# Gate and score matmuls of a hybrid decoder layer moved into two 64-row tiles of the array

## What is computed

```python
scores = einsum('bnqhgd,bnkhd->bnhgqk', qb, kc) * 64 ** -0.5       # each block of 128 queries against its own and the previous 128 keys
p = exp(scores - m); denom = sum(p) + exp(sink - m)                # a learned sink for each head
y_attn = rmsnorm(attention * silu(g_attn))

u = causal_depthwise_conv(x_lru)                                   # width 4
r = sigmoid(u @ w_r + b_r); i = sigmoid(u @ w_i + b_i)             # 16 blocks of 64 channels, block-diagonal
a = exp(-8 * r * softplus(-lam)); v = sqrt(1 - a * a) * (i * u)
h = scan(h = a * h + v)
y_lru = rmsnorm(h * silu(g_lru))
out = rmsnorm(x + concat([y_attn, y_lru]) @ w_out)
```

## Time and profile before

| | |
|---|---|
| median of three runs | 1438.38 us |
| the profiled execution, and its span | 1439.82 us, 1438.2 us |
| matmul records of TensorE | 6464, busy 96% of the span |
| VectorE, ScalarE, GpSimd busy | 71%, 53%, 22% |
| phase A, phase B | 1080 us, 358 us |
| clock granted to TensorE, as a share of full speed | 0.993 |

### The profile page before, as it was taken

One profiled execution on the slowest core, in us unless ns is written; L12 is line 12 of the kernel. 1 busy time (PEld: TensorE's weight loads), 2 busy tenths in 40 slices (PEclk: granted clock), 3 DMA queues, 4 the chain that ended last, 5 costly groups with the idle time before them and its releaser, 6 DMA issues.

```text
span 1438.2 us, 21776 instructions
## 1 busy us (share of the span) xinstructions
PE 1380.8 (96%) x6464; PEld 1136.5 (79%) x6464; DVE 1014.2 (71%) x1729; ACT 769.1 (53%) x1552; POOL 316.1 (22%) x317
## 2 busy tenths in 40 slices
PE   5999999799999999999999999999989999999997
PEld 4778777688888888888888878788868888888886
DVE  4798989687877778787787868777886644344443
ACT  5677685747475664747566564747575322222221
POOL 2131423042322314232231414232230000000000
PEclk9999999999999999999999999999999999999999
DMA  8767674755546454554636374544717323233220
GB/s 221 243 240 246 237 248 162 253 202 193 182 155 197 157 198 165 176 185 154 222 120 235 126 244 151 194 160 167 231 53 257 119 86 117 73 102 101 74 87 29
DMA packets 151726, 243.24 MB, mean 169 GB/s; under 512 B 35440, under 2 KB 101232, under 8 KB 151664
## 3 DMA queue, kind: packets, MB, share of 16 engines
q1 hardware_dynamic: 144496, 217.33, 45.4%
q0 software_dynamic: 7168, 25.17, 5.2%
HBM read 179.55 MB, written 62.91 MB: 169 GB/s over the span
## 4 chain that ended last, share of the span: by engine, by line
PE 43%; DVE 21%; issue 18%; ACT 8%; POOL 3%; DMA 2%; SPq 2%; DVEq 1%; ACTq 1%; POOLq 0%
PE ring L1408 18%; PE acc_b L201 12%; PE ring L201 11%; DVE hs L1283 5%; POOL ri L618 2%; DVE p_lo L1220 2%; ACT p_sb L834 2%; DVE s_sb L1194 2%; DVE smax L1207 1%; PE ps_v L1458 1%; DVE cu L1249 1%; DVE o_sb L1229 1%; ACT cu L858 1%; DVE w_lo L1002 1%; ACT kc_ol L847 1%
## 5 line engine op out<-in xcount | busy, mean ns | idle before, releaser
L1408 PE MATMUL ring<-split,w_hi 128*128 128x512 f32 x2304 | 720.3, 394 | 8.1 <-DVE split L1022 7.5
L1408 PEld LDWEIGHTS ring<-split,w_hi 128*128 128x128 f32 x2304 | 427.9, 189 | 95.6 <-DVE split L1022 8.4
L1408 PE MATMUL ring<-split,w_lo 128*128 128x512 f32 x1152 | 450.8, 391 | 0.0
L1408 PEld LDWEIGHTS ring<-split,w_lo 128*128 128x128 f32 x1152 | 217.2, 189 | 46.7
L834 ACT ACTIVATE p_sb<-s_sb,smax 128x129 f32<-128x129 f32 x256 | 99.9, 392 | 124.6 <-DVE smax L1207 124.4
L618 POOL TENSOR_TENSOR ri<-ri,hs 128x512 f32<-128x512 f32 x32 | 54.8, 1732 | 395.6 <-ACT hs L900 395.6
L774 ACT ACTIVATE q_st<-qrot 64x512 fp32r<-64x512 f32 x64 | 40.4, 631 | 114.9 <-DVE qrot L1085 114.1
L1249 DVE SCALAR_TENSOR_TENSOR cu<-xl,prm,cu 128x512 f32<-128x512 f32 x96 | 72.2, 752 | 39.6 <-ACT cu L858 30.6
L1669 ACT ACTIVATE w_hi<-res 128x1024 fp32r<-128x1024 f32 x16 | 17.0, 1061 | 144.5 <-DVE res L1728 144.5
L201 PE MATMUL ring<-split,y_own 128*128 128x512 f32 x384 | 91.3, 392 | 0.0
L201 PE MATMUL acc_b<-wo_rest,y_own 128*128 128x512 f32 x384 | 89.8, 390 | 0.5 <-DVE wo_rest L162 0.5
(11 more groups left out here) (195 smaller groups left out, 2486.0 us busy)
## 6 DMA issues: line engine op xcount, KB each, us to landing
w_hi<-w_split_scratch SPq DMA_DIRECT2D x108, 512.0 KB, 3.3
w_lo<-w_split_scratch SPq DMA_DIRECT2D x108, 512.0 KB, 4.3
w_split_scratch<-w_hi SPq DMA_DIRECT2D x36, 512.0 KB, 5.0
w_split_scratch<-w_lo SPq DMA_DIRECT2D x36, 512.0 KB, 5.7
w_raw<-w_in_d SPq DMA_DIRECT2D x32, 512.0 KB, 4.4
y_scratch<-hs POOLq DMA_DIRECT2D x32, 256.0 KB, 5.0
y_scratch<-ya POOLq DMA_DIRECT2D x16, 512.0 KB, 8.7
rows<-y_scratch SPq DMA_DIRECT2D x8, 1024.0 KB, 7.5
```

Of the source, the lines that this page charges most:

```text
L1408: last = mm(bank(r), w[:, i % WSLOTS, k, :], h[:, par, k, :], start=(k == 0 and j == 0), stop=(k == KC - 1 and j == 2))
```

## The change

The gate matmuls take 64 rows each. The lower 64 rows of the array hold, side by side, r and i of the first block of channels; the upper 64 rows hold i and r of the second. Three passes for two row tiles remain 6 matmuls of 512 columns, without the zeros. One bank then holds r below and i above (first block), the other i below and r above (second block), so that ScalarE takes each gate with two instructions of 64 rows. TensorE waits for both banks before the first pass, and ScalarE for both before the first tanh. For the first unit the halves of i are taken ahead of the decay, for the second behind it.

The score matmuls take one head in the lower and one in the upper 64 rows. q is split in place (`q_hi`, `q_lo`) with one instruction each, and a block has 12 matmuls of 256 columns (3 passes, 2 heads, 2 pairs) in place of 8; the product low·low falls away. The sinks are copied in two instructions, and the gate weights' two splits are half as wide.

```diff
-        q_st = sb("q_st", [P, GQ, T], F32R)
+        q_hi = sb("q_hi", [P, 2, T], F32R)
+        q_lo = sb("q_lo", [P, 2, T], F32R)
...
-        gw_raw = sb("gw_raw", [P, UNITS, 2, P])
+        gw_raw = sb("gw_raw", [P, UNITS, P])
...
+                        at = (j + half) % 2
+                        sp.dma_start(gw_raw[rows, :, at * BW:(at + 1) * BW],
...
             def high_q(n, j):
-                for half in range(2):
-                    rows = slice(half * HD, (half + 1) * HD)
-                    nc.scalar.activation(q_st[rows, 2 * j + half, :], qrot[rows, :], ACT.Copy
-                                         ).then_inc(*q_high.one())
+                nc.scalar.activation(q_hi[:, j, :], qrot[:, :], ACT.Copy).then_inc(*q_high.one())
...
                 def decays(u):
                     G = g * UNITS + u
-                    act.wait_ge(*ring_ready.at(n, (R_R0, R_R1)[u] + 1))
+                    lower, upper = slice(0, BW), slice(BW, P)
+                    first, second = bank(R_R[u]), bank(R_I[u])
+
+                    def take_i():
+                        for to, ps in ((lower, first[upper, :]), (upper, second[lower, :])):
+                            nc.scalar.activation(ri[u][to, :], ps, ACT.Tanh, scale=0.5,
+                                                 bias=prm[to, G, C_BI:C_BI + 1]).then_inc(*ring_act.one())
+
+                    act.wait_ge(*ring_ready.at(n, R_I[u] + 1))
                     act.wait_ge(*scanned.at(n, u + 1 - UNITS))
                     act.sem_inc(settled, 1)
-                    nc.scalar.activation(ra[u][:, :], bank((R_R0, R_R1)[u]), ACT.Tanh, scale=0.5,
-                                         bias=prm[:, G, C_BR:C_BR + 1]).then_inc(*ring_act.one())
-
-                    act.wait_ge(*ring_act.at(n, FREED_BY_ACT.index((R_R0, R_R1)[u]) + 1))
+                    for to, ps in ((lower, first[lower, :]), (upper, second[upper, :])):
+                        nc.scalar.activation(ra[u][to, :], ps, ACT.Tanh, scale=0.5,
+                                             bias=prm[to, G, C_BR:C_BR + 1]).then_inc(*gate_r.one())
+
+                    if u == 0:
+                        take_i()
+                    act.wait_ge(*gate_r.at(n, 2 * u + 2))
...
                     nc.scalar.activation(a2[:, :], ra[u][:, :], ACT.Square).then_inc(*decay.one())
-                    act.wait_ge(*ring_ready.at(n, (R_I0, R_I1)[u] + 1))
-                    act.sem_inc(settled, 1)
-                    nc.scalar.activation(ri[u][:, :], bank((R_I0, R_I1)[u]), ACT.Tanh, scale=0.5,
-                                         bias=prm[:, G, C_BI:C_BI + 1]).then_inc(*ring_act.one())
+                    if u == 1:
+                        act.sem_inc(settled, 1)
+                        take_i()
...
-                    for h in range(GQ):
-                        for k, st, sp_ in ((k_hi, True, False), (k_lo, False, True)):
-                            last = mm(ps_s[:, h, :], q_st[:, h, b * BLK:(b + 1) * BLK],
-                                      k[:, b * BLK:(b + 2) * BLK], start=st, stop=sp_)
+
+                    for j in range(2):
+                        for i, (v, k) in enumerate(((q_hi, k_hi), (q_hi, k_lo), (q_lo, k_hi))):
+                            for half in range(2):
+                                rows = slice(half * HD, (half + 1) * HD)
+                                last = mm(ps_s[:, 2 * half + j, :], v[rows, j, b * BLK:(b + 1) * BLK],
+                                          k[rows, b * BLK:(b + 2) * BLK], start=(i == 0), stop=(i == 2))
...
-                    for j in range(2):
-                        r = ((R_R0, R_I0), (R_R1, R_I1))[u][j]
-                        pe.wait_ge(*bank_free(n, r))
-                        for i, (w, v) in enumerate(((gw_hi, u_hi), (gw_hi, u_lo), (gw_lo, u_hi))):
-                            last = mm(bank(r), w[:, u, j, :], v[:, :], start=(i == 0), stop=(i == 2))
-                        last.then_inc(*ring_ready.one())
+
+                    for half in range(2):
+                        pe.wait_ge(*bank_free(n, (R_R, R_I)[half][u]))
+                    for i, (w, v) in enumerate(((gw_hi, u_hi), (gw_hi, u_lo), (gw_lo, u_hi))):
+                        for half in range(2):
+                            rows = slice(half * BW, (half + 1) * BW)
+                            ins = mm(bank((R_R, R_I)[half][u]), w[rows, u, :], v[rows, :], start=(i == 0), stop=(i == 2))
+                            if i == 2:
+                                ins.then_inc(*ring_ready.one())
```

More of the change, by code:

```diff
@@ L67 @@
 RING = 4
+R_R, R_I = (R_R0, R_R1), (R_I0, R_I1)
 RING_OF_GROUP = [R_XL0, R_GL0, R_XL1, R_GA0, R_GA1, R_GL1, R_KV, R_Q0, R_Q1]
@@ L280, in phase_a @@
         sink_all = sb("sink_all", [P, KV * GQ])
+        sink_pairs = sink_all[:, :].rearrange("p (j s) -> p j s", s=2)
         prm = sb("prm", [P, LRU_W // P, NPRM])
@@ L318, in phase_a @@
         h_carry = sb("h_carry", [P, LRU_W // P, 1])
-        gw_raw = sb("gw_raw", [P, UNITS, 2, P])
-        gw_hi = sb("gw_hi", [P, UNITS, 2, P], F32R)
-        gw_lo = sb("gw_lo", [P, UNITS, 2, P], F32R)
+        gw_raw = sb("gw_raw", [P, UNITS, P])
+        gw_hi = sb("gw_hi", [P, UNITS, P], F32R)
+        gw_lo = sb("gw_lo", [P, UNITS, P], F32R)
         ring = both.ring
@@ L372, in phase_a @@
         q_rot = signal("q_rot", 2, ahead=2)
-        q_high = signal("q_high", 4, ahead=4)
-        q_low = signal("q_low", 4, ahead=4)
+        q_high = signal("q_high", 2, ahead=2)
+        q_low = signal("q_low", 2, ahead=2)
         v_prev = signal("v_prev", 1, ahead=1)
@@ L385, in phase_a @@
         s_cap = signal("s_cap", 1)
-        s_sink = signal("s_sink", 1)
+        s_sink = signal("s_sink", 2)
         s_stat = signal("s_stat", NBLK)
@@ L411, in phase_a @@
         gw_low = signal("gw_low", 1)
+        gate_r = signal("gate_r", 2 * UNITS)
         decay = signal("decay", 3 * UNITS)
@@ L536, in _ @@
             load_consts()
-            sp.wait_ge(zeroed, 6)
+            sp.wait_ge(zeroed, 5)
             sp.wait_ge(pro_T, 2 * NBLK)
@@ L571, in body @@
                         rows = slice(half * BW, (half + 1) * BW)
-                        sp.dma_start(gw_raw[rows, :, j, rows],
+                        at = (j + half) % 2
+                        sp.dma_start(gw_raw[rows, :, at * BW:(at + 1) * BW],
                                      w[0, bass.ds(g * (2 * UNITS), 2 * UNITS), :, :].rearrange(
@@ L611, in _ @@
             pool.sem_inc(primed, 1)
-            for ap in (k_carry, v_carry[:, :, :], x_carry[:, :, :], h_carry[:, :, :], gw_raw[:, :, :, :]):
+            for ap in (k_carry, v_carry[:, :, :], x_carry[:, :, :], h_carry[:, :, :]):
                 nc.gpsimd.memset(ap, 0.0).then_inc(zeroed, 1)
@@ L905, in body @@
                 act.wait_ge(*ring_ready.at(n, R_I1 + 1 - NR))
-                nc.scalar.activation(gw_hi[:, :, :, :], gw_raw[:, :, :, :], ACT.Copy).then_inc(*gw_high.one())
+                nc.scalar.activation(gw_hi[:, :, :], gw_raw[:, :, :], ACT.Copy).then_inc(*gw_high.one())
                 if split:
@@ L1074, in turn_q @@
                 dve.wait_ge(*ring_act.at(n, FREED_BY_ACT.index((R_Q0, R_Q1)[j]) + 1))
-                dve.wait_ge(*q_low.at(n, 2 * j))
-                dve.wait_ge(*q_high.at(n, 2 * j))
+                dve.wait_ge(*q_low.at(n, j))
+                dve.wait_ge(*q_high.at(n, j))
                 dve.wait_ge(*(q_rot.at(n, j) if j else k_rot.at(n, 1)))
@@ L1088, in low_q @@
             def low_q(n, j):
[L1089 to L1095, removed]
+                dve.wait_ge(*q_high.at(n, j + 1))
+                nc.vector.tensor_tensor(q_lo[:, j, :], qrot[:, :], f(q_hi[:, j, :]), ALU.subtract
+                                        ).then_inc(*q_low.one())
             def previous_v(n, g):
@@ L1157, in _ @@
             dve.wait_ge(table_in, 32)
-            dve.wait_ge(zeroed, 6)
+            dve.wait_ge(zeroed, 5)
             turn_k(-1, 0)
@@ L1185, in sink_in @@
                     dve.wait_ge(*p_exp.at(n, 0))
-                    nc.vector.tensor_scalar(s_sb[:, :, :, BLK], sink_all[:, bass.ds(g * GQ, GQ)].unsqueeze(1)
-                                            .broadcast_to([P, 2, GQ]), 1.0, None, ALU.mult
-                                            ).then_inc(*s_sink.one())
+                    for half in range(2):
+                        ins = nc.vector.tensor_scalar(
+                            s_sb[:, :, 2 * half:2 * half + 2, BLK],
+                            sink_pairs[:, bass.ds(g * 2, 2), half].unsqueeze(1).broadcast_to([P, 2, 2]),
+                            1.0, None, ALU.mult)
+                        ins.then_inc(*s_sink.one())
                 def softmax_a(b):
@@ L1203, in softmax_a @@
                         dve.wait_ge(*s_cap.at(n, 1))
-                        dve.wait_ge(*s_sink.at(n, 1))
+                        dve.wait_ge(*s_sink.at(n, 2))
                     dve.sem_inc(settled, 1)
@@ L1226, in gather_o @@
```

(4 more changed lines are left out.)

## The result

The changed kernel takes 1476.49 us (median of four runs, 1474.34 to 1478.32) against 1439.22 us for the kernel before in the same comparison: a ratio of 1.0259, 95% interval 1.0241 to 1.0277. It is slower by 37 us. The forecast was 1460, range 1445 to 1486: the side and the mechanism came out, the size was too small. The spans of the two profiled executions differ by 34.5 us (1472.7 against 1438.2), and it is these that the rows divide up; the changed kernel's is the shortest of its four (1474.34).

A forecast was written before the change was run, and what follows sets the result against it. A ScalarE, GpSimd, VectorE chain about as long as TensorE's work was taken to bound the kernel; its growth of 4.8, 11.4 and 5.6 us, together 21.8, took the profiled 1439.8 to 1461.6, median 1460 us, range 1445 to 1486.

The forecast's parts named there:

- The bound: From XL1's end to weigh_v(3), a ScalarE, GpSimd, VectorE chain is as long as TensorE's own work, to 0.4 us.
- Overlap of the tiles: On TensorE, gates and score: two row tiles running at the same time would save 37.8 us of work.
- the rival without overlap: TensorE's row tiles don't overlap: gates 1.40, score 1.43, 3 us more an iteration, about 1487 us; chance 0.08.
- Weight loads: In TensorE's score, loads follow one after another at 0.11 us: 1.32 us, 0.37 more than before; overlapping loads give 0.71.
- The switch: TensorE's change between 128-row and 64-row matmuls: 8 an iteration, 128 in all, each between nothing and about 0.35 us.
- The rival: TensorE drains at every change of tile size: with 0.3 us each, 2.4 us an iteration, 1473 us; chance 0.22.
- ScalarE's part: Two more tanh per decays at 0.57 us a step: decays(0) 0.7 us longer, decays(1) 1.14 us longer.
- The overlap of one half with the next on ScalarE: Rival: halves overlap on ScalarE, the chain doesn't grow, TensorE's saving counts where there is room: 1433 us; chance 0.11.
- The sum: Over all iterations: first quarter 4.8 us, second and third 11.4, fourth 5.6, together 21.8 us more.
- Cover: high_q, low_q, sinks and narrower splits lie under three projections of TensorE, between gather_o(2) and the next gates(0), costing nothing else.
- a credit in the first quarter's head: At the iteration's head VectorE gets back 2 x 0.6 us from low_q and 0.26 from the narrower split; up to 0.95 usable.

The follow-up runs named there:

- The halves without the tiles: The kernel before, with only the four tanh of decays each taken in two instructions of 64 rows, no matmul changed: 1485.75 us, ratio 1.0322.
- The tiles without the halves: The changed kernel with each bank's tanh in one instruction of 128 rows; mixes up r and i, for its time alone: 1430.75 us, ratio 0.9936.
- the kernel with the copy on VectorE: The changed kernel with the copy of block 1's scores out of PSUM moved from ScalarE to VectorE in quarters 2 to 4: 1470.99 us, ratio 1.0211.
- The scores alone in tiles: The kernel before with only the edits of score, q and the sinks; gates and tanh as before: 1434.97 us, ratio 0.9967.
- the single half of i shown above: From the changed kernel with the first unit's last half tanh of i moved behind u_hi; the remaining half of i ahead of the decay: 1473.68 us, ratio 1.0234.

## Why the prediction was right, and where it was too small

- **The bound.** Right. The prediction held that a chain over ScalarE, GpSimd and VectorE is as long as TensorE's work to 0.4 us, so that TensorE's saving can hardly show and any growth of the chain does. The halves without the tiles cost 46 us. The tiles without the halves gave 1.9 us in the two middle quarters, for which the bound was worked out (328.68 to 837.33, before 331.98 to 842.50), where TensorE's own balance, half of 37.8 us less 64 switches of 0.19, was 6.7.
- **Overlap of the tiles.** Right; the rival without overlap is out, with a pair of 512 columns in 0.23 us.
- **Weight loads.** Wrong: I took them one after another, 0.11 us each, from a row of loads of 128 rows. The loads of a pair start as one, and `score` takes 0.71 us and not 1.32. The rule of the Trainium skill that I had weighed against the row was right (TensorEngine Tiling (Array Packing), Tiling Modes: different tiles can load weights and multiply in parallel); the trace agrees, with 0.12 us a pair. This term was 0.6 us too high for each score. By my own sum the right term gives 1457 in place of 1460, 3 us further from the measured time.
- **The switch.** The rival put it at 0 to 0.35 us and my sum at nothing. It is 0.19 us, 0.09 of it before the first matmul and 0.10 before the second. The Trainium skill's rule (TensorEngine Tiling (Array Packing), Key Properties: a change of mode drains TensorE) agrees with the trace as far as this stall; whether the array runs empty in it, no row shows. All 128 cost 24 us of TensorE's time and 37.8 are saved, so its own work is still 13 us shorter. To make up the 37 us they would have had to cost 0.59 us each, (37.3 + 37.8) / 128. That the rival's 1473 lies nearer to the measured time than my 1460 is chance: with every switch and no half tanh the kernel takes 1430.75.
- **ScalarE's part** is the term that was mis-sized. I took 0.57 us for a half tanh, the step behind an activation of 128 rows; it is 0.71. The trace of the kernel before had the number. I took the length of the 64-row records from it and not their step. The two halves of q (rows below this list) are 0.63 us long and take 509.18 - 507.87 = 1.31 us to the next start, 0.655 each: a record and 0.02 more, where behind 128 rows the step is mostly a record less 0.10 us. A tanh of 0.69 us comes by this to 0.71. So `decays(0)` grew by 1.33 us (forecast 0.7) and `decays(1)` by 1.54 (1.14). In the rows: `score(0)` to `gates(1)` +0.71 us (forecast 0.3); `gates(1)` to the scan 491.86 - 480.56 = 11.30 against 9.70, +1.60 (1.14). An iteration of the second quarter takes 472.03 - 405.85 = 66.18 us, 2.4 more; the forecast was 1.4. The overlap of one half with the next on ScalarE, which would have made the change faster, was none: the halves stand 0.71 us apart.
- **The sum.** 7.8, 18.8 and 7.8 us for the first quarter, the two in the middle and the last, against 4.8, 11.4 and 5.6. The ratio is 1.6 in the first three quarters and 1.4 in the fourth, so an iteration grew by 2.35 us in the middle and by 1.95 at both ends. The first quarter's figure is the least firm: the kernel with the copy on VectorE has the same lists there and takes 283.0 us for it, 2.0 more than the changed kernel.
- **Cover.** I called `high_q` and `low_q` covered, apart from a credit in the first quarter's head. The scores alone in tiles came out 4.5 us faster in spite of the extra time on TensorE. Up to the second quarter it is 3.3 us ahead, which fits that credit; the 2.4 us of its fourth quarter I had not counted.

The two halves of q in the kernel before, and what follows them (timeline of ScalarE):

```profile
507.87 1.28 ACT L774 ACTIVATE q_st<-qrot 64x512 fp32r<-64x512 f32 x2 [4.22 <-DVE qrot L1085]
509.18 0.60 ACT L758 ACTIVATE qraw<-ring 128x512 f32<-128x512 f32 x1
```

The scan at the end of the chain in the changed kernel (timeline of VectorE; compare), with a wait of 1.26 us for GpSimd, before 1.28:

```profile
489.32 1.28 DVE L1030 SCALAR_TENSOR_TENSOR rows<-rows,x_stat 128x1024 f32<-128x1024 f32 x1
491.86 2.21 DVE L1296 TENSOR_TENSOR_SCAN hs<-ra,h_carry,ri 128x512 f32<-128x512 f32 x1 [1.26 <-POOL ri L625]
...
496.90 0.68 DVE L1233 TENSOR_TENSOR p_lo<-ps_t,p_hi 128x512 fp32r<-128x512 f32 x1
```

What stays open: why the changed kernel with the copy on VectorE has iterations of two lengths in its middle quarters, and why ScalarE starts the next instruction before the end of one half of i and of no other half. Neither was followed up.

## What to carry to other kernels

A busy share of 96% doesn't say that the engine alone sets the pace: follow one iteration through all engines and write down the room at each place where they meet, before counting what a saving is worth. Packing an array by rows moves the results about, and here ScalarE, which takes them out, paid for each row range with an instruction as long as a full one; count how the results are taken out before the matmuls. For a price on an engine, read the distance between two starts, not the length of a record. Where two chains are equally long, try the parts of a change one by one: here the scores and q in place gave TensorE more to do and were still worth keeping, with one copy moved to an idle engine.

## What the runs showed of the hardware that I had not expected

- Two matmuls of 64 rows in different halves of the array, with their weight loads, start as one: a pair of 256 columns in 0.12 us, a pair of 512 in 0.23, in float32r.
- Between matmuls of 128 rows and of 64 rows, either way, 0.19 us was lost: 0.09 before the first and 0.10 before the second.
- An activation of 64 rows and 512 columns on ScalarE lasts as long as one of 128 rows (0.68 us for the tanh). In the kernel before and in the changed one, whatever came right behind an activation of 64 rows started 0.02 to 0.03 us after its end; behind 128 rows the next one of 128 rows mostly started 0.1 us before the end. The one exception is the single half of i shown above, with a step of 0.59 us. A tanh of a whole bank thus cost 0.57 us, in row halves 1.42, in column halves 0.72.
